# Per-tile norms at the ends of phases, a joined route-and-plan stage and early expert weights, in a two-block transformer kernel

## What is computed

```
mod = silu(c) @ ada_w[i] + ada_b[i]            # six rows of 1024: sh1 sc1 g1 sh2 sc2 g2
h = rmsnorm(x, norm_g[i,0]) * (1 + sc1) + sh1
x = x + g1 * mixers(h)                         # i=0: convolutions, i=1: two attentions
h = rmsnorm(x, norm_g[i,1]) * (1 + sc2) + sh2
x = x + g2 * moe(h)                            # 32 experts of width 512 in 4 groups, 2 per token
return rmsnorm(x, final_norm_g)
```

## Time and profile before

| what | us |
|---|---|
| median of three runs | 4270.36 |
| lowest and highest | 4267.33, 4281.91 |
| the profiled execution's own time | 4277.79 |
| its span, first to last instruction | 4275.7 |
| TensorE busy (86% of the span) | 3662.3 |
| VectorE busy (40%) | 1707.6 |
| ScalarE busy (17%) | 743.8 |
| GpSimd busy (4%) | 177.4 |

### The profile page before, as it was taken

How to read it: one execution, slowest core, us unless ns; L and a number is a source line. 1 busy time by engine, 2 the same in 40 slices (tenths; PEclk the granted TensorE clock), 3 DMA queues, 4 the chain that set the end, 5 groups by cost and what they waited for, 6 DMA issues and landing times. The chain is left out here.

```text
span 4275.7 us, 40723 instructions
## 1 busy us (share of the span) xinstructions
PE 3662.3 (86%) x15948; PEld 1980.2 (46%) x15948; DVE 1707.6 (40%) x3100; ACT 743.8 (17%) x1432; POOL 177.4 (4%) x239
## 2 busy tenths in 40 slices
PE   7998899888999988988699599999387787699995
PEld 3453435873444433686244444444143443444442
DVE  2245556663314645675365201010558534210102
ACT  2132222000114312200010111111230322111111
POOL 0001110001000010000000000000000210000001
PEclk9999999998999999998899699999778899699998
DMA  2215441004211262101321399998441311499996
GB/s 83 79 40 197 149 129 40 1 1 140 88 50 45 65 197 83 30 1 57 123 100 38 125 429 429 429 429 379 136 131 29 111 35 45 176 429 429 429 429 259
DMA packets 200340, 704.48 MB, mean 165 GB/s; under 512 B 21416, under 2 KB 100776, under 8 KB 172560
## 3 DMA queue, kind: packets, MB, share of 16 engines
q1 hardware_dynamic: 174288, 610.25, 36.7%
q0 software_dynamic: 25920, 92.47, 6.1%
HBM read 655.92 MB, written 46.74 MB: 164 GB/s over the span
## 5 line engine op out<-in xcount | busy, mean ns | idle before, releaser
L299 PE MATMUL bank<-fm,w 128*128 128x512 f32 (+1 forms) x704 | 304.0, 593 | 0.0
L381 PEld LDWEIGHTS bank<-pick,experts_h 128*128 128x128 f32 x2368 | 272.5, 195 | 36.1 <-issue 28.4
L2607 PE MATMUL bank<-wd,hidT 128*64 128x512 f32 x1120 | 248.1, 595 | 45.1 <-ACT hidT L2650 45.1
L381 PE MATMUL bank<-pick,experts_h 128*128 128x128 f32 x2368 | 279.6, 280 | 7.2 <-DVE pick L2659 7.2
L2607 PE MATMUL bank<-wu,hs 128*64 128x512 f32 x1120 | 248.0, 595 | 15.6 <-DMA wu<-in_moe_w_up 15.5
L2607 PE MATMUL bank<-wg,hs 128*64 128x512 f32 x1120 | 251.0, 601 | 9.1 <-DMA wg<-in_moe_w_gate 9.1
L2678 DVE TENSOR_TENSOR y<-bank,mod 128x512 f32<-128x512 f32 x70 | 45.1, 686 | 528.3 <-PE bank L2607 528.3
L663 PE MATMUL bank<-fm,side_w 128*128 128x512 f32 x512 | 248.2, 610 | 6.7 <-DMA side_w<-in_w_in 5.3
L299 PE MATMUL bank<-w,fm 128*128 128x512 f32 (+1 forms) x512 | 213.9, 580 | 11.4 <-DMA w<-in_w_in 11.4
L299 PE MATMUL bank<-o_fm,w 128*128 128x512 f32 x384 | 178.8, 629 | 47.9 <-DMA w<-in_w_pb 19.3
L299 PEld LDWEIGHTS bank<-fm,w 128*128 128x128 f32 (+1 forms) x704 | 130.1, 185 | 172.9 <-issue 171.1
(11 more groups left out here) (459 smaller groups left out, 5112.0 us busy)
## 6 DMA issues: line engine op xcount, KB each, us to landing
wg<-in_moe_w_gate SPq DMA_DIRECT2D x70, 2048.0 KB, 15.9
wu<-in_moe_w_up SPq DMA_DIRECT2D x70, 2048.0 KB, 19.9
wd<-in_moe_w_down SPq DMA_DIRECT2D x70, 2048.0 KB, 17.3
ada_w<-in_ada_w POOLq DMA_DIRECT2D x96, 512.0 KB, 4.8
w<-in_w_in SPq DMA_DIRECT2D x48, 512.0 KB, 4.1
w<-in_w_in SPq DMA_DIRECT2D x20, 1024.0 KB, 7.4
expert_rows<-y POOLq DMA_DIRECT2D x35, 512.0 KB, 10.3
side_w<-in_w_in SPq DMA_DIRECT2D x32, 512.0 KB, 3.9
```

Of the source, the lines that this page charges most:

```text
L299: ins = pe.matmul(bank, lhsT, rhs, start=(n == 0), stop=(n == len(todo) - 1))
L381: last = pe.matmul(out, lhsT, rhs, start=(n == 0), stop=(n == len(pairs) - 1))
L2607: ins = pe.matmul(bank[rows, :], lhs[:, k, rows], weights[s][:, k, cols], start=(k == 0), stop=(k == chunks - 1))
```

## The change

It is one change with these parts.

1. `norm_to_fm` becomes the class `TileNorm`: squares, mean, root, norm, transposes (`turn`) and copies (`move`) of one tile at a time, with two buffers for the normed tile. Transposes go by tile into a pair of banks. Where a gain is applied, the copies are on VectorE, else on ScalarE.
2. Each norm stands in the stage that finishes x. At the start it runs while tables load; x comes in four loads. In `merge_out` it is behind the last four jobs, turns 0 and 1 ahead of the jobs for tiles 2 and 3; the phase has four banks for seven; `ada.add_up` moves one job up; after layer 1, the modulation rows are loaded and scaled in the same stage. In the out stages of the mixers and in `moe_residual` it follows each tile's last addition.
3. The mixers' output banks go in tile order, and the second mixer's weights in the order of their first use. The router's weights and bias are loaded during the mixer, its products (`score`) and the bias are part of the out stage.
4. `route` and `plan` are one stage. Its SP list loads the weights of experts 0 and 1. The plan gives each expert one block at its own number, and further blocks behind number 31, so that the first pair is always experts 0 and 1; it has some ten small instructions more. The loop on SP starts at pair 1.
5. The stages `clear`, `modulation`, `final_norm` and `end` go. Their work is in `moe_residual`, `conv_mixers`, `position_bias` and `merge_out`. The output is stored by tile.

The core of the diff (in `TileNorm`, `ready(t)` is the semaphore value at which tile t of x is complete):

```diff
+    def take_dirty(self):
+        used, self.dirty = self.dirty, []
+        self.cleared = used + self.cleared
         for c in self.cleared:
             c.total = 0
+        return used
...
-def norm_to_fm(chip, x, fm, finish, rows=None, normed_tm=None):
...
+class TileNorm:
...
+    def squares(self, act, t):
+        act.wait_ge(*self.ready(t))
+        if t:
+            act.wait_ge(*self.squared.at(t))
+        act.activation(self.junk, self.x[:, t, :], ACT.Square, accum_out=self.ss[:, t:t + 1]).then_inc(*self.squared.inc())
+    def ask(self, dve, t):
+        r = self.ss[:, t:t + 1]
+        dve.wait_ge(*self.squared.at(t + 1))
+        dve.tensor_scalar(r, r, 1.0 / D, EPS, ALU.mult, ALU.add).then_inc(*self.asked.inc())
+    def root(self, act, t):
+        r = self.ss[:, t:t + 1]
+        act.wait_ge(*self.asked.at(t + 1))
+        act.activation(r, r, ACT.Sqrt).then_inc(*self.rooted.inc())
+    def norm(self, dve, link, t):
+        r, x = self.ss[:, t:t + 1], self.x[:, t, :]
+        dve.wait_ge(*self.rooted.at(t + 1))
+        link(dve.reciprocal(r, r))
...
+        if t >= 2:
+            dve.wait_ge(*self.turned.at(t - 1))
...
+    def turn(self, pe, t):
+        pe.wait_ge(*self.normed.at(t + 1))
+        if t >= len(self.pairs):
+            pe.wait_ge(*self.moved.at(2 * (t - len(self.pairs) + 1)))
+        src = self.xn[:, t % 2, :] if self.dealt_to is None else self.dealt_to[:, t, :]
...
+    def move(self, eng, t):
+        eng.wait_ge(*self.turned.at(t + 1))
+        for n, bank in enumerate(self.banks(t)):
+            dst, src = self.fm[:, 4 * n:4 * n + 4, t * P:(t + 1) * P], bank[:, :].rearrange("p (k s) -> p k s", k=4)
+            if self.gain is None:
+                ins = eng.activation(dst, src, ACT.Copy)
+            else:
+                ins = eng.tensor_tensor(dst, src, over(self.gain[:, 4 * n:4 * n + 4], [P, 4, P], 2), ALU.mult)
+            ins.then_inc(*self.moved.inc())
...
+        halves[0][0].first = lambda pe, moved: pe.wait_ge(*moved(DC - 1))
+        for job in halves[0]:
+            job.ahead = lambda dve, moved: ada.weigh(dve, 3)
+        norm, prepare, load_rows = next_norm(st, lambda t: moved(DC + TILES + t))
+        link = st.chain(chip.nc.vector, "norm_step")
...
+        def behind(t):
+            def ahead(dve, moved):
+                if t == 0:
+                    ada.finish(dve, 0)
+                norm.ask(dve, t)
+                norm.norm(dve, link, t)
+                if t == 2 and norm.gain is not None:
+                    norm.move(dve, 0)
+            return ahead
+        def second_turn(pe, moved):
+            pe.wait_ge(*ada.added.at(1))
+            norm.turn(pe, 1)
+        halves[1][0].ahead = first_ahead
+        for t in range(TILES - 1):
+            halves[1][t + 1].ahead = behind(t)
+        halves[1][0].first = lambda pe, moved: ada.add_up(pe, 0)
+        halves[1][2].first = lambda pe, moved: norm.turn(pe, 0)
+        halves[1][3].first = second_turn
+        moved, done = phase(chip, st, work.loads, work.jobs, slots=3, banks=4)
         ada.load(st, done(0))
...
+            norm.turn(pe, 2)
+            norm.turn(pe, 3)
+            norm.ask(dve, 3)
+            norm.norm(dve, link, 3)
+            if norm.gain is not None:
+                for t in range(1, TILES):
+                    norm.move(dve, t)
...
+class Routed:
...
+    def score(self, pe, t):
+        if t == 0:
+            pe.wait_ge(*self.landed.at(32))
+            pe.wait_ge(*self.out_moved.at(5))
+        pe.wait_ge(*self.norm.moved.at(2 * t + 2))
+        n_r = GROUPS + EXPERTS
+        product(pe, self.chip.bank[4][:, t * n_r:(t + 1) * n_r], [(self.fm[:, k, t * P:(t + 1) * P], self.rw[:, k, :]) for k in range(DC)]
+                ).then_inc(*self.scored.inc())
...
+            for n in range(4):
+                self.store(dve, n)
+            for t in range(TILES):
+                norm.ask(dve, t)
+                norm.norm(dve, link, t)
+                if t in (0, 2):
+                    for n in (t + 4, t + 5):
+                        self.store(dve, n)
...
+            for t in range(TILES):
+                norm.squares(act, t)
+                norm.root(act, t)
+                if t >= 1:
+                    norm.move(act, t - 1)
+            norm.move(act, TILES - 1)
...
+        order = [(half, t) for t in range(TILES) for half in range(2)]
...
+            routed.load(sp, io, 0)
+            modulation_rows(chip, 1, mod, 0, 2, sp, spread)
...
+                routed.turn(pe, n - 6)
+            for t in range(TILES):
+                routed.score(pe, t)
+                if t + 2 < TILES:
+                    routed.turn(pe, t + 2)
...
+            modulation_rows(chip, 1, mod, 2, 6, sp, spread)
+            sp.dma_start(gain[:, :], io["norm_rows"][3:4, :].to_broadcast([P, D])).then_inc(*spread.inc(16))
...
+            pieces = [cols_of(io["cd_w_out"][0], half * BANK, BANK)(out_w[half]) for half in range(2)]
+            for i in range(2):
+                for half in range(2):
+                    sp.dma_start(*pieces[half][i]).then_inc(*out_landed[half][i].inc(16))
+            routed.load(sp, io, 1)
 
...
+        more = SEQ // SLOTS - 1
+        link(dve.tensor_tensor(t3[:, :, 0:more], over(total, [P, E, more], 2), over(chip.block_starts[:, 1:], [P, E, more], 1), ALU.is_gt))
+        link(dve.tensor_reduce(blocks[:, :], t3[:, :, 0:more], AX.X, ALU.add))
...
+        link(dve.tensor_scalar(at_expert[:, :], chip.numbers[:, 0:E], float(SLOTS), None, ALU.mult))
+        link(dve.tensor_scalar(blocks[:, :], first[:, :], float(E - 1), float(SLOTS), ALU.add, ALU.mult))
+        link(dve.tensor_tensor(blocks[:, :], blocks[:, :], at_expert[:, :], ALU.subtract))
+        link(dve.tensor_scalar(over_one[:, :, :], ranks, float(SLOTS), None, ALU.is_ge))
+        link(dve.tensor_tensor(over_one[:, :, :], over_one[:, :, :], over(blocks[:, :], [P, TILES, E], 1), ALU.mult))
+        link(dve.tensor_scalar(slot[:, :, :], routed[:, :, :], 1.0, -FAR, ALU.subtract, ALU.mult))
+        link(dve.tensor_tensor(slot[:, :, :], slot[:, :, :], ranks, ALU.add))
+        link(dve.tensor_tensor(slot[:, :, :], slot[:, :, :], over(at_expert[:, :], [P, TILES, E], 1), ALU.add))
+        dve.tensor_tensor(slot[:, :, :], slot[:, :, :], over_one[:, :, :], ALU.add).then_inc(*placed.inc())
...
+        dve.tensor_copy(hot[:, 0:E], chip.ident[0:E, 0:E]).then_inc(*taken.inc())
...
-            with sp.Fori(0, n) as p:
+            with sp.Fori(1, n) as p:
...
+            with chip.stage("route_and_plan") as st:
+                choice, routed = st.sb("choice", [P, 2, TILES, EXPERTS]), st.sb("routed", [P, TILES, EXPERTS])
+                routed_ready = st.count("routed_ready")
+                weights_loaded = [st.count(n, fresh=True) for n in ("gate_loaded", "up_loaded", "down_loaded")]
+                @st.block.sync
+                def _(sp):
+                    for name, pair, loaded in zip(("moe_w_gate", "moe_w_up", "moe_w_down"), weights, weights_loaded):
+                        for s in range(2):
+                            sp.dma_start(pair[s][:, :, :], io[name][i, s].rearrange("(p k) n -> p k n", p=P)).then_inc(*loaded.inc(16))
+                route(chip, st, lg, choice, weight, routed, routed_ready)
+                plan(chip, st, choice, routed, routed_ready, slot_of, row_of, counts)
+            item_experts(chip, i, io, h, slot_of, counts, mod[:, 5, :], made, weights, weights_loaded)
...
+                for c in used:
+                    sp.sem_clear(c.sem)
+                if last_layer:
+                    sp.dma_start(g[:, :], io["norm_rows"][2 * DEPTH:2 * DEPTH + 1, :].to_broadcast([P, D])).then_inc(*gain_loaded.inc(16))
+                    for t in range(TILES):
+                        sp.wait_ge(*norm.normed.at(t + 1))
+                        sp.dma_start(out[0, t * P:(t + 1) * P, :], rows[:, t, :]).then_inc(*stored.inc(16))
+                    sp.wait_ge(*stored.at(16 * TILES))
...
+                for t in range(TILES):
+                    add_rows(dve, t)
+                    norm.ask(dve, t)
+                    finish(t)
...
+                for t in range(TILES):
+                    norm.squares(act, t)
+                    norm.root(act, t)
+                    if t and not last_layer:
+                        norm.move(act, t - 1)
+                if not last_layer:
+                    norm.move(act, TILES - 1)
...
+def first_norm(chip, x, fm, gain, landed, consts_landed):
+    with chip.stage("first_norm") as st:
+        xn, junk = st.sb("xn", [P, 2, D]), st.sb("junk", [P, D])
+        norm = TileNorm(chip, st, x, fm, lambda t: landed[t].at(16), [(0, 1), (2, 3), (4, 5), (6, 7)], xn, junk[:, :], gain=gain)
+        @st.block.scalar
+        def _(act):
+            for t in range(TILES):
+                norm.squares(act, t)
+                if t >= 1:
+                    norm.root(act, t - 1)
+            norm.root(act, TILES - 1)
...
```

(13 more changed lines are left out.)

663 lines of the change are left out of this document (319 added, 344 removed).

## The result

The changed kernel takes 4125.26 us (median of four runs, 4121.34 to 4129.70), the kernel before 4270.47 (four runs, 4267.33 to 4281.91): ratio 0.9656, 95% interval 0.9635 to 0.9676. The forecast was 4132.9, the range 4110 to 4160. So it is 145.2 us faster where 137.5 were forecast. The profiled execution has a span of 4127.8 us against 4275.7.

A forecast was written before the change was run, and what follows sets the result against it. Bound by seven serial chains between phases, with the expert loop bound by DMA: 7.0 + 9.8 + 31.3 + 34.5 + 16.1 + 33.6 + 5.2 = 137.5 us off 4270.4 gives 4132.9, range 4110 to 4160.

The forecast's parts named there:

- Seven serial chains: Stretches between phases, 397.9 us together, each ended by one serial chain; the change is worth what these chains lose.
- Start: Start to first product: norms run per tile while the tables load, first product at 27.3 instead of 34.34, 7.0 us saved.
- both merges: First w_out product to first product of the next phase: 9.8 us saved after layer 0, 31.3 after layer 1.
- the rows beside the ada weights: Layer 1's merge: 5 MB of modulation row loads on SP's queue beside POOL's ada weights, cost taken as 0.
- its own list: Wrong if merges wait for ada weights, the loop's period changes from its second pair, or the clock stays low into it.
- Fronts: Last output product to first gate product: 31.3 us saved in layer 0, 30.4 in layer 1, first weight wait included.
- Loops: Expert loops, bound by DMA: early first weights save 6.5 us a layer, 3.3 of it the first wait.
- rivals 2 and 3: Early expert weights buy nothing, 4146 us (chance 0.06), or buy the whole load, 29.3 for 6.5 per layer, 4087 (0.02).
- Rival 4: Expert loop: clock stays low, 26 us more per pair; with seven pairs 4315 us, slower than before; chance 0.02.
- Experts to attention: Last y store of layer 0 to the position bias: clearing stage gone, norms tile by tile, 16.1 us saved.
- End: Last y store to the end: clearing stage gone, adds and norms per tile, output stored by tile, 5.2 us saved.
- Rival 1: New in-order waits on one engine in out phases, merge and residuals cost 25 us in all: 4158 us; chance 0.12.

## Why the prediction was right

**The bound.** Seven serial chains between phases, and phases that keep their length: right. The stretches named gained 147.6 together, the whole table 146.1; the rows between them are small (-0.9, -1.9, 0.3, -1.9) or chance (3.0 of the attention), and the conv mixer kept its 202. Whether layer 1's body kept its length is open, as said above. Undone one by one were the early weights, the tile order and the place of the turns, and the start was run alone; that the rest of the merges' and fronts' gain comes from the shorter chains rests on the traces, step by step, and on no run of its own.

**Start, both merges.** 7.3, 10.4 and 31.6 for 7.0, 9.8 and 31.3. The walk held nearly step by step: a turn in the stream cost 0.87, not 1.45, at the clock that was up there (granted 1.00), and turn 3 of layer 1's merge cost 1.97, not 1.4, at 0.50, since it had fallen by then. The terms of the way to the conv mixer add up to 15.75 and not to the 16.1 of the prediction; measured are 13.6 behind the stream, 1.7 for the turns and 0.97 for the late weighing, 16.3. The rows that I put at 5 MB are 4.2. On the rows beside the ada weights two sources spoke against each other: I took 0 for their cost, and worked out 3 from the Trainium skill (DMA: Bandwidth & Descriptors, "Issuing engines are not separate DMA queues"). Its mechanism is right: VectorE waited 11.9 us, and 0.4 with most of the rows taken away; before the change no weighing in w_out's stretch waited. The price was 0.3 to 1.0 on TensorE's path, since the weighing had nearly that much slack. By its own list the prediction would be wrong if VectorE or TensorE waited for ada weights in the merge. Both did: the step that no weighing would be late was wrong, and only its price was near the 0 that I took.

**Fronts.** 32.8 and 34.8 for 31.3 and 30.4. The path behind the last product had three terms wrong. From there to route it is 16.2 in layer 0, for 18.3. The turns: I had all four behind the last product, 5.7; turn 0 stands ahead of the last bank's products (2304.77), and the other three took 3.4. The scores: I had 3.0 for each tile, between the low clock's 3.47 and a full one, 12.0; each took 1.87 for tiles 0 and 1, right behind the stream at a granted clock of 1.00, and 3.44 for tiles 2 and 3 at 0.50, 10.5 on the path. Against that, TensorE waited 1.8 for the norm of tile 3, where I had no wait: the norm, and not TensorE, sets the end, though it came 6.9 behind the last product and not the 9.2 of my walk. So the sum came out nearer than its terms. In layer 1 turn 3 (0.93) and the last two scores (5.66) ran faster, as the clock came back during them, and route began 14.2 behind the last product. Plan and route cost 1.5 more than before, for 1.2.

**Loops.** The forecast was 6.5 a layer for the early weights; undoing them cost 8.9 and 10.1 (front and loop together). Missing was the first gate product: I left it at 9.45, the price of the earlier trace rows, and the wait that went took its cause along. The periods went as worked out in kind (the queue rests until the first products are done, at 2375.7, then 30.56 again): 3.2 and 2.9, with the first up weights, for 3.2. Five of them were 29.9 and not the eight of the prediction, which its own 3.2 did not allow: 0.7 saved in each of five is 3.5. (Its upper bound for a loop is loose, too: 17 x 0.7 is 11.9, not 11.) That run excludes rivals 2 and 3. Rival 4 did not come: in every trace with the early load the first gate product took 7.09; without it the clock was lower over that product alone, the up product behind it took 7.09.

**Experts to attention.** 15.7 for 16.1, but with a loss behind it that I didn't have: the rows moved into the position bias hold up its small loads, 1.9 us (0.2 with the wait added). That is the step I failed to follow: a moved DMA was costed on the queue it left, not on the one it came to. A table load was 1.28 and there was one for each residual stage, as forecast; the 2.7 of the Trainium skill (ScalarE: Activation LUTs, "Table sets: the hidden batching unit") did not show: the root behind it began 1.3 us after the square's sum was read.

**End.** 3.6 for 5.2: taking the clearing of counts out of its own stage gave 1.2 (last store to first gather 5.6 instead of 6.8), not 2.8. In layer 0 it was 1.1, and there the other steps made up for it.

**Rival 1** was right in kind only: late ada weights and late small loads cost 0.97 and 1.9, 3 us of its 25. TensorE's waits for the norm of tile 3 (1.8 in each out stage) were outweighed by cheaper turns and scores. The order that avoids the rest was in the change, as the run with the turns behind shows.

**What is luck.** In one pair of traces the attention alone would have moved the result by 11 us either way; the medians agree with the sum of the chains because they average over it. Misses of both signs met as well: the fronts gave 5.9 and the loops 5.0 more than forecast, the end 1.6 and the small loads 1.9 less. The range of 50 us was wider than the chains needed (they missed by 0.3 to 4.4 each, 8.6 in all with the stretches put at 0), and about right once that spread is counted.

## What to carry to other kernels

Between two phases the price is the serial chain from the last product to the next one; write it down for the last tile alone, since all earlier tiles fit behind the stream if no in-order engine makes them wait. A wait that goes may take the low clock of the product behind it along: here that was over a quarter of what the early load gave (2.5 and 2.9 of 19). When a load is moved, look at what else is in flight where it arrives; and when a wait for weights is named, ask what else ends at the same time, before taking it as the gain. Look also at what stands behind it on the same queue: the index weights, put ahead of the bias's stores, delayed those.

## What the runs showed of the hardware

- The same masked attention, edited in none of the kernels, takes 77.7 to 93.2 us (352 products, granted clock 0.90 and 0.81) in thirteen traces of eleven kernels, and in the kernel before alone 93.2 and 84.0. The bodies of the layers spread from 961.8 to 966.9 and from 969.1 to 973.7. In both most of the difference arises at the hand-over into an attention, which takes 10.8 to 14.7 us: four products there took 0.64 in one trace and 1.09 in another, after the same waits of 0.7 to 0.8. So two single spans can't be compared to better than some 15 us here, while most of the other stretches repeat to 1 us. Exceptions are front 0 (54.4 to 56.0) and, in the kernel before, the last store of layer 0 to the memset (58.0 and 60.1).
- Broadcast rows of 4.2 MB on SP's queue held up 0.5 MB loads of the POOL queue by 11.9 us in sum (11.0 in the same kernel's second trace); 1.6 MB by 0.4. What is late is not in proportion to the bytes.
